# Constant products on TensorE during the first load, and the first norm's work dealt out to three engines

## The reference

```python
h = jnp.concatenate([meta, x], axis=1)
for i in range(DEPTH):
    u = rms_norm(h, mix_norm_g[i])          # x * rsqrt(mean(x*x) + eps) * g
    h = h + mixer_i(u, ...)                 # layer 0: conv + pool, layer 1: gated linear attention
    u = rms_norm(h, ffn_norm_g[i])
    h = h + squared_relu_mlp(u, ...)        # 4096 wide
return rms_norm(h[:, N_META:], final_norm_g)
```

## Time and profile before

| | us |
|---|---|
| median of 3 runs | 1107.34 |
| lowest, highest | 1106.65, 1107.49 |
| span of the profiled execution | 1105.6 |
| TensorE busy in that span | 1091.0 |

### The profile page before, as it was taken

One profiled execution on the slowest core, in us unless ns is written; L12 is line 12 of the kernel. 1 busy time (PEld: TensorE's weight loads), 2 busy tenths in 40 slices (PEclk: granted clock), 3 DMA queues, 4 the chain that ended last, 5 costly groups with the idle time before them and its releaser, 6 DMA issues.

```text
span 1105.6 us, 18616 instructions
## 1 busy us (share of the span) xinstructions
PE 1091.0 (99%) x7649; PEld 1019.9 (92%) x7649; DVE 811.0 (73%) x1166; ACT 562.8 (51%) x933; POOL 4.6 (0%) x34
## 2 busy tenths in 40 slices
PE   7999999999999999999999999999999999999997
PEld 6999999999999999999999788787898898899897
DVE  6889987786786785789463456756796786786885
ACT  6658455454454454466642234534464454454564
POOL 1000000000000000000000000000000000000000
PEclk9999999999999999999999999999999999999999
DMA  7321122135134124223223211223134134234221
GB/s 213 116 76 49 58 76 88 40 115 152 39 115 129 63 83 146 77 77 114 77 78 95 75 61 39 69 84 110 43 115 147 45 115 123 68 100 130 77 76 78
DMA packets 98929, 100.39 MB, mean 91 GB/s; under 512 B 2834, under 2 KB 95692, under 8 KB 98844
## 3 DMA queue, kind: packets, MB, share of 16 engines
q1 hardware_dynamic: 98780, 99.12, 28.5%
q10 hardware_dynamic: 64, 0.07, 0.0%
HBM read 97.09 MB, written 2.10 MB: 90 GB/s over the span
## 4 chain that ended last, share of the span: by engine, by line
PE 97%; DVE 1%; ACT 0%; DMA 0%; issue 0%; DVEq 0%; ACTq 0%
PE ps L1876 56%; PE ps L2080 27%; PE ps L2151 4%; PE ps L2009 2%; PE ps L2232 2%; PE ps L1923 1%; PE ps L2247 1%; PE ps L2112 1%; PE ps L2181 1%; PE ps L1884 1%; DMA xin<-in_x_dram 0%; PE ps L2139 0%; DVE w_lo L577 0%; DVE sq_sum L1267 0%; PE ps L2271 0%
## 5 line engine op out<-in xcount | busy, mean ns | idle before, releaser
L1876 PE MATMUL ps<-u_lo,w_hi 128*128 128x264 f32 (+1 forms) x1120 | 298.9, 322 | 1.0 <-DVE u_lo L1328 1.0
L1876 PE MATMUL ps<-u_hi,w_hi 128*128 128x264 f32 (+1 forms) x1120 | 295.3, 320 | 0.0
L1876 PE MATMUL ps<-u_hi,w_lo 128*128 128x264 f32 (+1 forms) x1120 | 294.6, 319 | 0.0
L2080 PE MATMUL ps<-c_lo,w_hi 128*128 128x264 f32 (+1 forms) x868 | 245.9, 283 | 0.6 <-DVE w_lo L577 0.6
L2080 PE MATMUL ps<-c_hi,w_hi 128*128 128x264 f32 (+1 forms) x868 | 244.9, 282 | 0.0
L2080 PE MATMUL ps<-c_hi,w_lo 128*128 128x264 f32 (+1 forms) x868 | 244.7, 282 | 0.0
L1876 PEld LDWEIGHTS ps<-u_lo,w_hi 128*128 128x128 f32 x1120 | 184.9, 188 | 19.6 <-issue 4.2
L531 ACT ACTIVATE w_hi<-raw 128x1024 fp32r<-128x1024 f32 x118 | 123.7, 1056 | 151.8 <-PE ps L1876 134.1
L1876 PEld LDWEIGHTS ps<-u_hi,w_hi 128*128 128x128 f32 x1120 | 185.8, 188 | 16.0 <-issue 0.7
L1876 PEld LDWEIGHTS ps<-u_hi,w_lo 128*128 128x128 f32 x1120 | 185.6, 188 | 15.4
L538 DVE TENSOR_TENSOR w_lo<-raw,w_hi 128x1024 fp32r<-128x1024 f32 x118 | 143.6, 1222 | 76.5 <-ACT w_hi L531 74.4
(11 more groups left out here) (266 smaller groups left out, 1374.5 us busy)
## 6 DMA issues: line engine op xcount, KB each, us to landing
raw<-in_ffn_w_dram SPq DMA_DIRECT2D x64, 1024.0 KB, 5.4
raw<-in_gla_w_in_dram SPq DMA_DIRECT2D x12, 1024.0 KB, 5.3
raw<-in_cp_w_in_dram SPq DMA_DIRECT2D x8, 512.0 KB, 5.3
raw<-in_cp_w_out_dram SPq DMA_DIRECT2D x4, 1024.0 KB, 5.0
raw<-in_gla_w_out_dram SPq DMA_DIRECT2D x4, 1024.0 KB, 5.2
xin<-in_x_dram SPq DMA_DIRECT2D x4, 512.0 KB, 5.6
raw<-in_cp_w_in_dram SPq DMA_DIRECT2D x2, 1024.0 KB, 5.0
out_dram<-y_tok SPq DMA_DIRECT2D x4, 512.0 KB, 3.1
```

The costliest lines, as they stand in the source:

```text
L1876: last = mm(ps[:, n % NS, c:c + b - a], l, r[:, a - origin:b - origin], start=(k == 0 and i == 0), stop=(k == count - 1 and i == 2))
L2080: last = mm(bank, l[:, 0, j, :], r, start=(fresh and j == 0 and m == 0), stop=(j == KD // 2 - 1 and m == 2), skip_group_check=not fresh)
```

## The change

It has five parts.

1. GpSimd fills `ones_d` first and reports it on a semaphore of its own (`ones_ready`).
2. TensorE makes 10 products of `ones_d` with itself (128 x 128, float32, plain) into an unused PSUM slot as soon as `ones_d` is there, and 4 more behind `flip_meta(0)`. No one reads them.
3. The square and sum of token tile 1 moves from ScalarE to VectorE, which does it ahead of the first reciprocal; ScalarE waits for it (`second_squared`) before the root of tile 1.
4. The scaling of the meta tokens moves from VectorE to GpSimd; TensorE waits for it (`meta_normed_ready`) ahead of `flip_meta(1)`.
5. TensorE's transposes are put in another order: 6 of tile 0, the normed meta tokens, 6 of tile 1, 6 of tile 2, then channel tiles 6 and 7 of the tiles 0 to 2, then the 8 of tile 3.

```diff
-        N_CONST = 14
+        N_CONST = 13
+        WARM = (10, 4)
...
+            pool.memset(ones_d[:, :], 1.0 / D).then_inc(ones_ready, 1)
             pool.memset(ident[:, :], 0.0).then_inc(consts, 1)
...
-            pool.memset(ones_d[:, :], 1.0 / D).then_inc(consts, 1)
...
+            pool.wait_ge(meta_loaded, 16)
+            pool.wait_ge(rstd_tok_ready, 2)
+            pool.tensor_scalar(meta_normed, xmeta[:, :], rstd_tok[0:META, TT:TT + 1], None, ALU.mult)\
+                .then_inc(meta_normed_ready, 1)
...
             for j in range(TT):
-                act.wait_ge(x_loaded[j], 16)
-                act.activation(squares, xin[:, j, :], ACT.Square, accum_out=ms_tok[:, j:j + 1])\
-                   .then_inc(x_squared, 1)
-                act.wait_ge(x_squared, j + 1)
+                if j == 1:
+                    act.wait_ge(second_squared, 1)
+                else:
+                    act.wait_ge(x_loaded[j], 16)
+                    act.activation(squares, xin[:, j, :], ACT.Square, accum_out=ms_tok[:, j:j + 1])\
+                       .then_inc(x_squared, 1)
+                    act.wait_ge(x_squared, max(j, 1))
...
+            dve.wait_ge(x_loaded[1], 16)
+            V.scalar_tensor_tensor(out=x_normed[:, 1, :], in0=xin[:, 1, :], scalar=1.0, in1=xin[:, 1, :],
+                                   op0=ALU.mult, op1=ALU.mult, accum_out=ms_tok[:, 1:2]).then_inc(second_squared, 1)
             for i, t in enumerate((0, TT, 1, 2, 3)):
                 rows = META if t == TT else P
                 dve.wait_ge(x_std, i + 1)
                 V.reciprocal(rstd_tok[0:rows, t:t + 1], std_tok[0:rows, t:t + 1]).then_inc(rstd_tok_ready, 1)
+                if t == TT:
+                    continue
                 dve.wait_ge(rstd_tok_ready, i + 1)
-                src, dst = (xmeta[:, :], meta_normed) if t == TT else (xin[:, t, :], x_normed[:, t, :])
-                V.tensor_scalar(dst, src, rstd_tok[0:rows, t:t + 1], None, ALU.mult).then_inc(x_normed_ready, 1)
+                dve.wait_ge(x_loaded[t], 16)
+                V.tensor_scalar(x_normed[:, t, :], xin[:, t, :], rstd_tok[:, t:t + 1], None, ALU.mult)\
+                 .then_inc(x_normed_ready, 1)
...
+            def warm_up(count):
+
+                for _ in range(count):
+                    mm(ps[:, NS - 1, 0:P], ones_d[:, :], ones_d[:, :], start=True, stop=True)
+
+            pe.wait_ge(ones_ready, 1)
+            warm_up(WARM[0])
             pe.wait_ge(consts, N_CONST)
...
             flip_meta(0, xmeta)
+            warm_up(WARM[1])
             pe.wait_ge(x_normed_ready, 1)
             for k in range(KD - 2):
                 flip_normed(0, k)
-            pe.wait_ge(x_normed_ready, 2)
+            pe.wait_ge(meta_normed_ready, 1)
             flip_meta(1, meta_normed).then_inc(filled_n, 1)
-            pe.wait_ge(x_normed_ready, 3)
-            for k in range(KD - 2):
-                flip_normed(1, k)
-            for j in range(2):
+            for j in range(1, TT - 1):
+                pe.wait_ge(x_normed_ready, j + 1)
+                for k in range(KD - 2):
+                    flip_normed(j, k)
+            for j in range(TT - 1):
                 for k in (KD - 2, KD - 1):
                     flip_normed(j, k)
-            for j in range(2, TT):
-                pe.wait_ge(x_normed_ready, j + 2)
-                for k in range(KD):
-                    flip_normed(j, k)
+            pe.wait_ge(x_normed_ready, TT)
+            for k in range(KD):
+                flip_normed(TT - 1, k)
```

More of the change, by code:

```diff
@@ L343, in build_trunk @@
         meta_squared = sem("meta_squared")
+        second_squared = sem("second_squared")
+        meta_normed_ready = sem("meta_normed_ready")
         gain_turned = sem("gain_turned")
@@ L358, in build_trunk @@
         consts = sem("consts")
+        ones_ready = sem("ones_ready")
         filled_n = sem("filled")
```

## The result

| | before | changed |
|---|---|---|
| median (8 runs each) | 1107.37 | 1110.26 |
| lowest, highest | 1106.65, 1107.56 | 1109.41, 1110.50 |
| span of the profiled execution | 1105.6 | 1107.9 |

The ratio is 1.0025, 95% interval 1.0016 to 1.0035: slower by 2.9 us, where I had forecast faster by 1.1. The profiled execution took 1109.72 us, the third fastest of the eight.

The account below looks back on a forecast made before the run. TensorE, busy 1091.0 of 1105.6 us, bounds the kernel; only the first projection's start counts. From 16.77 to 15.7 gains 1.1: 1107.34 - 1.1 = 1106.2 us, range 1105.0 to 1108.5.

Parts of the forecast that it names:

- The rigid shift: Behind the first projection TensorE has hardly a gap, so an earlier or later S moves the end by as much.
- S: Start of the first projection on TensorE, 16.77 us before the change; forecast at 15.7, a gain of 1.1.
- Part 2, cost: Constant products in the head: 20 passes, 4.3 us from 1.0 to 5.3, and 8 more, all hidden at no cost.
- M: Time at which GpSimd's scaled meta tokens are ready; forecast 10.7, between 9.65 and 11.85.
- the sum behind M: Transposes and the steps after them up to the first projection, at full clock: S = M + 5.0.
- let the clock stay up: The forecast case in the head: clock up and kept, gain 1.1, time 1106.2, chance 0.57.
- The half-clock formula: Transposes at half clock throughout: S = M + 7.35, so S 17.3 to 19.2, a loss of 0.5 to 2.4.
- the second: Rival: clock up and lost again, or up late, in the head; gain 0, time 1107.3, chance 0.20.
- the third: Rival: clock not raised for the transposes; price 1.3, time 1108.6, at worst 1109.7, chance 0.18.
- half of 20 transposes: Price of a lost clock behind the meta tokens: half of the 20 transposes at 0.21 costs 1.1.
- A row that I read too loosely: Granted clock at the kernel's end: its fall from 1.00 to 0.50 was taken to follow thin work.
- The range: Total time 1105.0 to 1108.5, said to leave out no more than 2 in 10.

Follow-up runs that it names:

- experiment 8: Kernel before with only the meta scaling moved from VectorE to GpSimd; 1110.05 us, ratio 1.0024.
- experiment 5: Kernel before with the constant products, their constant filled first, and the new order of transposes, no norm work moved; 1105.39 us, ratio 0.9984.
- experiment 9: Changed kernel with the square of token tile 1 back on ScalarE; 1106.69 us, ratio 0.9998.
- experiment 4: Kernel before with eight GpSimd scalings of 16 x 1024 added, one after the other; no scaling under 2.8 us, its own total time says nothing.
- experiment 6: Changed kernel with 8 instead of 4 products ahead of tile 0 and 13 new ones in the wait for GpSimd; 1109.69 us, ratio 1.0015.
- experiment 11: Kernel before with only the new order of the transposes; 1107.12 us, ratio 0.9999.
- experiment 1: Changed kernel with the meta scaling back on VectorE; 1106.12 us, ratio 0.9997.
- experiment 10: Changed kernel with the meta scaling back on VectorE and 8 instead of 4 products ahead of tile 0; 1105.93 us, ratio 0.9993.

## Why the prediction was wrong, by its own steps

- **The rigid shift held.** S alone moved: 2.29 us against 2.3 of the span. The profiled executions of the other timed experiments agree within 0.2 us; experiment 8 does not, by 1.0 us.
- **Part 2, cost.** Right: 20 passes in 4.64 us from 0.99, hidden ahead of the gain rows, though only just (they end at 5.6, forecast 5.3); 8 more hidden ahead of tile 0 where the clock is up. At half clock they aren't quite: in experiments 5 and 9 tile 0 had to wait for them until 8.6 and 8.7.
- **Part 3.** Its direct size was about right: tile 0 at 8.48, forecast 8.56. What I missed is that this opens a pause of 1.05 us (7.43 to 8.48) right behind the raised clock. I had named the pause in a rival, but given no price to part 3 for it. Alone, part 3 costs 1.1 us; taken out of the changed kernel, it gives back 3.6.
- **Where the miss lies.** S was forecast at 15.7 and came at 19.06, 3.4 later. M, the end of GpSimd's scaling, was 1.35 late; the sum behind M was 0.3 short; and 1.7 came from transposes at half clock.
- **Part 4, the mis-sized cost.** I priced the scaling at 1.3 us from a fill and an affine select, plus 0.75 for one conflict, 2.05 in all, so M = 10.7. It took 3.37 and M was 12.05, beyond my upper end of 11.85. Experiment 4 gives 2.83 where nothing is in the way, experiment 8 the same. So 1.5 us was missing in the operation, and the conflict was 0.5. Neither row was a fair stand-in: a fill reads nothing, and a select of 128 columns is short and of another kind. (Scaled in full, 8 x 0.29, the select would have given 2.3.)
- **Behind M, the sum.** I had S = M + 5.0 at full clock. Experiment 9 ran all 28 transposes at full clock and has S - M = 15.95 - 10.63 = 5.3: the 28 take 3.0 us, not 2.65. So with M = 12.05 even a kept clock gives S = 17.4, a loss of 0.6: the sign of my forecast hung on the price of part 4.
- **The clock, the larger share.** The other 1.7 us are the same 28 transposes at 4.71 instead of 3.01 us. In the forecast I let the clock stay up, at 0.57. In none of eight executions did the changed kernel come to what that would give. The half-clock formula, M + 7.35, gives 19.4 for this M; a few of the last transposes ran at full clock. Of the rivals it is thus the second in its mechanism (up and lost) with nearly the third's worst price. I had set its price from "half of 20 transposes" at M = 10.7. In the profiled execution the clock fell at 9.0, behind the pause that part 3 opens, and it stayed down through the wait for M. So the late tile, the late M and the low clock come together, and the chances should have been given to the three as one case. Experiment 6 points the same way from the other side: in its fast group, kept busy, the same GpSimd scaling gives 1108.15.
- **A row that I read too loosely.** I took the fall at the end of the kernel before for one "after work as thin as this". TensorE's last instruction there ends at 1099.9, and the column is at 1.00 until 1100.9 and at 0.50 from 1101.1 on. The clock fell while TensorE stood still, 1.1 us behind its last work, so this row says nothing about thin work.
- **Part 5.** Neutral alone (experiment 11), and worth 0.3 us beside the products (1105.39 against 1105.69, with overlapping intervals). The pause for the meta columns' bank is gone in experiment 5's profile: the last 26 transposes follow each other there.
- **The range** ended at 1108.5. I had S up to 19.2, 1109.7, in the text, and gave its case too little weight.

Of the Trainium skill's rule on transposes (TensorE: Matmul & The Clock Gate, Part 4: PE-mode transpose), experiment 1 says what the trace of before said: in 10.0 to 13.4 us TensorE did transposes alone and the clock stayed at 1.00. What goes with the loss of the clock here is a pause of TensorE: with it filled, the group that had lost the clock was gone (experiment 10).

## What to carry to other kernels

An operation that the trace doesn't show on an engine should be measured there before it is put in front of an engine that waits in order; here the meta scaling cost 0.74 us on one engine and 2.8 to 3.4 on the other. Products that raise TensorE's clock pay (1.4 us here, 2.0 with the new order) if real work follows them closely; a change that delays that work can also take back the clock, so the two must be priced together. The constant products with the new order, and no norm work moved, is the version to keep: 1105.39 us, ratio 0.9984 against the kernel before.

## What the runs showed of the hardware

- GpSimd's scaling by a per-row scalar in float32 took 2.84 us for 1024 columns and 1.57 for 512, with 128 rows no slower than 16. The Trainium skill (GPSIMD Engine Reference, section 4.1, Engine selection) has one-input operations on GpSimd at roughly line rate; the trace disagrees, with 2.84 us against VectorE's 0.74 for the same tile, 3.8 times as long.
- GpSimd and VectorE slow each other: scalings of 0.75 us on VectorE took up to 1.42, and GpSimd's 2.84 up to 3.9. Who pays differs: in experiments 8 and 9 GpSimd kept its 2.84 and VectorE took 1.03 and 1.40.
- The moment at which the granted clock rises differs between executions by several us: in the profiled ones of experiment 1, the changed kernel and experiment 5 it rose at 4.5, 5.6 and 10.0 us, with the same ten products in front. In the profiled ones of experiments 6 and 9 it rose at 10.5 and between 10.2 and 10.7. Together with whether the clock is lost again, this gives one kernel two groups of times (1105.7 to 1106.2 and 1108.1 to 1108.5 in experiment 1), and a median can jump between them.
